# Moving rows of the split products placed 32 bytes later in each partition

## What is computed

```python
# first block: 16 meta tokens ahead of the 512, L = 528
h = h + mixer(rmsnorm(h))                      # hgrn2 scan and latent attention
h = h + relu(rmsnorm(h) @ up0) ** 2 @ down0    # first perceptron, 1024 -> 4096 -> 1024
h = h + multiscale_pool(rmsnorm(h))
h = h + relu(rmsnorm(h) @ up1) ** 2 @ down1    # second perceptron; from here on 512 tokens count
# second block
y = concat(gated_delta_rule(u @ w_in), memory_attention(q_mem, mem_k, mem_v)) @ w_out
h = h + rmsnorm(y)
h = h + rmsnorm((silu(x @ w_g) * (x @ w_u)) @ w_d)   # gated perceptron (ffn), 1024 -> 2816 -> 1024
```

## Time and profile before

| | |
|---|---|
| time, median of 3 runs | 1866.42 us (1862.13 to 1869.57) |
| the profiled execution's own time | 1862.51 us |
| its span, first to last instruction | 1860.4 us |
| mean granted TensorE clock | 0.996 |
| busy: PE, PEld, DVE, ACT | 98%, 89%, 70%, 50% |

### The profile page before, as it was taken

The page is one execution under the profiler, slowest core; times in us unless marked ns, Lnnn a source line. Parts: engine busy times, 40 slices in busy tenths (PEclk is TensorE's granted clock), DMA queues, the critical chain, the costliest instruction groups (busy, mean ns, idle before and its releaser), DMA issues.

```text
span 1860.4 us, 31132 instructions
## 1 busy us (share of the span) xinstructions
PE 1817.1 (98%) x12498; PEld 1658.4 (89%) x12498; DVE 1308.8 (70%) x1882; ACT 925.1 (50%) x1557; POOL 33.1 (2%) x31
## 2 busy tenths in 40 slices
PE   7999999999999999999999999999999999999997
PEld 7888878999999999898899878787889898999996
DVE  4664476767777776877777768778738379877775
ACT  5456444544334446654344433645667464544553
POOL 0100001200000000000000000000000000000000
PEclk9999999999999999999999999999999999999998
DMA  5211101232233232333233322222200422333331
GB/s 198 71 57 58 60 1 46 80 100 94 91 92 113 80 119 89 105 102 103 91 104 105 103 97 92 80 69 80 80 1 33 139 80 91 114 103 102 109 108 56
DMA packets 63364, 162.55 MB, mean 87 GB/s; under 512 B 4632, under 2 KB 29464, under 8 KB 63096
## 3 DMA queue, kind: packets, MB, share of 16 engines
q1 hardware_dynamic: 62368, 158.59, 25.9%
q10 hardware_dynamic: 856, 2.00, 0.3%
HBM read 156.38 MB, written 4.19 MB: 86 GB/s over the span
## 4 chain that ended last, share of the span: by engine, by line
PE 86%; DVE 7%; ACT 3%; DMA 2%; DVEq 1%; issue 1%; SPq 0%; ACTq 0%
PE ps L722 73%; PE ps L1405 2%; DMA USLF<-W 1%; PE ps L945 1%; PE ps L1425 1%; DVE wlo L3400 1%; PE ps L1274 1%; DVE wlo L3030 1%; PE ps L920 0%; PE ps L1410 0%; PE ps L1253 0%; PE ps L1251 0%; ACT WU L2638 0%; DMA H<-xT 0%; PE ps L921 0%
## 5 line engine op out<-in xcount | busy, mean ns | idle before, releaser
L722 PE MATMUL ps<-UH,whi 128*128 128x264 f32 (+1 forms) x696 | 202.8, 291 | 9.6 <-DVE wlo L3030 9.6
L722 PE MATMUL ps<-USH,whi 128*128 128x512 f32 (+1 forms) x584 | 209.2, 358 | 0.8 <-DVE USL L3944 0.7
L722 PE MATMUL ps<-USL,whi 128*128 128x512 f32 (+1 forms) x584 | 201.8, 345 | 0.0
L722 PE MATMUL ps<-UL,whi 128*128 128x264 f32 (+1 forms) x696 | 198.1, 285 | 0.0
L722 PE MATMUL ps<-UH,wlo 128*128 128x264 f32 (+1 forms) x696 | 197.7, 284 | 0.0
L1965 ACT ACTIVATE whi<-raw 128x1024 fp32r<-128x1024 f32 x114 | 119.3, 1052 | 83.1 <-PE ps L722 63.1
L722 PE MATMUL ps<-KFH,whi 128*128 128x264 f32 x512 | 145.7, 285 | 1.6 <-DVE KFL L3442 1.5
L722 PE MATMUL ps<-KFH,wlo 128*128 128x264 f32 x512 | 145.3, 284 | 0.0
L722 PE MATMUL ps<-KFL,whi 128*128 128x264 f32 x512 | 145.2, 284 | 0.0
L722 PEld LDWEIGHTS ps<-UH,whi 128*128 128x128 f32 (+1 forms) x696 | 130.9, 188 | 10.9 <-issue 9.8
L722 PE MATMUL ps<-TH,whi 128*128 128x256 f32 x504 | 139.1, 276 | 0.0
(11 more groups left out here) (588 smaller groups left out, 5079.5 us busy)
## 6 DMA issues: line engine op xcount, KB each, us to landing
raw<-W SPq DMA_DIRECT2D x134, 512.0 KB, 3.5
raw_p<-W SPq DMA_DIRECT2D x46, 1024.0 KB, 5.0
ULF<-W SPq DMA_DIRECT2D x22, 512.0 KB, 4.0
USLF<-W SPq DMA_DIRECT2D x22, 512.0 KB, 4.0
raw_d<-W SPq DMA_DIRECT2D x14, 512.0 KB, 3.9
H<-xT SPq DMA_DIRECT2D x4, 528.0 KB, 6.7
spill<-H SPq DMA_DIRECT2D x1, 2048.0 KB, 7.0
H<-spill SPq DMA_DIRECT2D x1, 2048.0 KB, 8.6
```

The costliest lines, as they stand in the source:

```text
L722: mm = pe.matmul(dst, a, b, start=start and n == 0, stop=stop_ and n == 2, skip_group_check=again)
```

## The change

Both bases go up by 32 bytes; every tensor laid out from them moves along, and the order of the instructions on every engine stays word for word the same.

```diff
-        us_at = u_at + 320
+        us_at = u_at + 352
         assert us_at + 2 * KT * SEQ * 4 <= u_at + 2 * KT * L * 4
...
-        S0 = base[0]
+        S0 = base[0] + 32
```

## The result

The changed kernel takes **1885.89 us** (median of 3, 1883.81 to 1887.3) against 1866.42: ratio **1.0098, 95% interval 1.0074 to 1.0121**, slower by 1%. The forecast was 1869 and its range ended at 1881.

What follows compares the result with a forecast made beforehand. The prediction took TensorE's pace on L722 to bound the kernel; +5.1 us for 256 columns and -2.7 us for 512 gave +2.4 us on the median of 1866.42, so 1869 us, with a range of 1854 to 1881.

Steps and rivals of the forecast that it cites:

- What bounds the kernel: Whole kernel: TensorE, busy 98% of the span, sets the time by its pace on L722, the split product.
- I take it for all: 256-column products on L722: the 116.7 ns seen at start 160 is assumed for every one at 224.
- The 256-column term: 256-column products on L722: 1,920 fast ones lose 3.35 ns, 1,240 slow ones gain 1.1 ns, together +5.1 us.
- 512 columns, -1.1 ns: 2,460 products of 512 columns on L722: half the lower bound taken, -2.7 us; bounds 5.4 us each way.
- The sum: Whole kernel: +5.1 - 2.7 = +2.4 us, +0.13%, giving 1869 us on the median.
- "faster" rival: L722 products: 224 has the fast lock at both widths, 113.3 and 226.7 ns; -10.9 us, 1855.5; chance 25%.
- Everything else: First region's 264-column products, plain float32 products, VectorE, ScalarE and weight pieces landing in USLF: 0 change.
- "slower" rival: L722 products: rows at 224 touch one more 64-byte block, 117.8 and 231.1 ns; +13.9 us, 1880; chance 28%.
- "Nothing": L722 products: the lock depends on when a run begins, not where its row does; 1866; chance 10%.
- third lock: Sign of a wrong forecast: L722 products at 224 run at a pace that is no neighbour of the known ones.
- The count of 1,920 and 1,240: 256-column products on L722 in the trace before: 1,920 counted at 113.3 ns and 1,240 at 117.8 ns.

Runs made afterwards that it cites:

- the table: Moving rows put at each of eight starts modulo 256, weights unmoved, against the kernel before; medians from 1866.42 us (192, the kernel before) to 1885.89 us (224, the change).
- the first profile: The kernel before, nothing changed, as profiled for the prediction; the profiled execution took 1862.5 us.
- the second: The kernel before, nothing changed, profiled once more; 1870.49 us.
- the third: The kernel before, nothing changed, profiled a third time; 1860.42 us.
- three kernels of this kind: Against the kernel before, 512-column hidden rows moved to distance 0: all, 1867.76 us; only high parts, 1872.46 us; only rests, 1875.03 us.
- a fourth: All 512-column hidden rows at distance 0 and USH and USL moved there too, against the kernel before; 1868.34 us, ratio 1.0009.

## Why the prediction was wrong

- **What bounds the kernel**: right. The whole difference is the distance of starts on L722, and reading it from long stretches was the right instrument: the same subtraction gave every pace of the table.
- **"I take it for all", 116.7 from 160**: the step that failed, with the next. The 256-column term was +5.1 us with an upper bound of 117.8. Measured is 120.0: 1,920 x 6.7 + 1,240 x 2.2 = +15.6 us by the prediction's own counts. 116.7 is what 160 costs, and it does so for `TH` as well; but 160 is 32 from the weights' start and 224 is 96 from it. Being off a multiple of 64 was the wrong likeness.
- **512 columns, -1.1 ns, "bounds -2.2 and +2.2"**: wrong in sign, and the upper bound did not hold. Measured is +4.4 ns in long runs, 2,460 x 4.4 = +10.8 us in place of -2.7. The bound was a run with two rows in three at 160 and one at 192; a mix is no bound for its parts, all at 160 take 233.3. The lean downward came from three products in a stretch that steps through eight starts; it had no bearing on a run that holds one start. The bound could have been read from the trace of before: two runs of 23 products of 512 columns at 192 went at 233.3, not 228.9, in it (22 distances in 5.13 us by the unrounded starts). The first and last start of one of them (the other is from 924.28 to 929.42 us):

```profile
788.10 0.40 PE L722 MATMUL ps<-MFL,whi 128*128 128x512 f32 x1
...
793.24 0.40 PE L722 MATMUL ps<-MFH,wlo 128*128 128x512 f32 x1
```

- **The sum**: 15.6 + 10.8 = 26.4 us by paces, 21.4 in the spans. Both traces hold the same 12,498 products in the same order, so start can be set against start: from 759 us on the products of 256 columns take 15.4 us more and those of 512 columns 9.8 (4.0 ns each, for many of their short runs went at 229.3 to 230.1 before), the waits take 2.9 us less, and what lies ahead of 759 us 0.9 less: 21.4. About half of the waits lie in the second perceptron's middle, where TensorE stood idle for 209.68 - 208.38 = 1.3 us before and 0.2 after. The prediction counted with such waits only as lost gain in its "faster" rival; they soften a loss too.
- **"Everything else" at 0**: holds within a microsecond for the stages before 759 us; VectorE, ScalarE and the transfers of 4.0 and 4.1 us were cover as said.
- **The "slower" rival**, 1880: right in sign, wrong in mechanism (no 64-byte block decides) and short by 6 us, since it was priced with the same two bounds. "Nothing" fell, and "faster" too; against both stand 120.0 and 233.3 in every run. The list of what would make the forecast wrong named a third lock that is no neighbour of the known ones. That is what came: 120.0 and 233.3 stand in no line of its list of paces (113.3, 116.7, 117.8; 226.7, 228.9, 231).
- **The count of 1,920 and 1,240, from one execution**: it was that execution's, not the kernel's. Against the first profile the change costs 21.3 us, against the second, with its ffn pairs at 117.8, 1884.05 - 1870.49 = 13.6, and against the third 23.6. Part of the change's cost is thus that it never has the good draw: at distance 96 only 120.0 was seen.

The Trainium skill's gap of N / 2.4 + 2.5 ns ("TensorE: Matmul & The Clock Gate", section "Back-to-back issue gap") is 109.2 and 215.8 ns here; no place of the table reaches it, the best are 4 and 11 ns above. The section itself calls this the gap of an isolated matmul, and for a stream with a weight load to each product it gives about 131 ns at 512 columns; the trace doesn't agree with that either, 226.8 ns is the least of the table. Its 16-byte lines ("SBUF — State Buffer", section "Specifications (TRN2)") can't tell these starts apart, while the runs do.

Open: what the two reads share. The runs show that the distance between the moving row's and the weights' start counts, modulo 256 bytes, and make it likely that a run's pace also hangs on the products ahead of it; they show neither the part of the chip in which the two meet nor what picks a run's pace where a distance has two. All weights' blocks begin at one place modulo 512, so whether a product's own weights count or the next one's, loaded meanwhile, wasn't tried.

## What to carry to other kernels

Where each product loads new weights, the start of the moving row against the start of the weights is a tuning knob worth 1% here: try the eight places of 32 bytes, for each width by itself, and keep the distance when either is moved. Don't price an unseen place by a likeness or by a run that mixes places. And before counting how many products run at which pace, compare two or three executions: a spread of times that is wide for one layout and narrow for another was here the sign of a pace drawn anew.

## What was not expected of the hardware

- Two kernels with all rows and weights 32 bytes apart run alike (113.3 and 228.9 ns at distance 64), while a shift of one operand alone costs up to 6.7 ns a product.
- The best distance differs by width: 64 for 256 columns (113.3 ns), 0 for 512 (226.8 ns in long runs), where 256 columns take 120.0.
- At distance 64 a run of 256 columns holds one of two paces, 113.3 or 117.8 ns, through 252 products, and unchanged code draws it anew: 6.2 us between the ffn stages of two executions (from the start of the first pair to that of the last two, 235.4 and 229.2 us). At distances 128 and 160 the paces (118.6 and 120.0, 118.6 and 117.4) come in a fixed order from pair to pair.
- The rows ahead seem to decide for those behind: with the hidden rows of 512 columns at distance 0, the 32 pairs, at distance 64 as before, all took 117.8. One profile each of three kernels of this kind speaks for it, and the 18 ffn pairs of a fourth; how it comes about isn't shown.
